# Mixture-of-experts decoder step: shift rows added by VectorE, and the last expert's rows picked on TensorE while the other experts' rows are gathered

## The reference

```python
    x = x + g1 * mixed
    h2 = (rms_norm(x, p['norm2_w']) * (1 + sc2) + sh2).reshape(bt * s, D_MODEL)
    comb = route(h2, w_router, router_bias)
    y_moe = moe_ffn(h2, comb, p['w_exp_gate'], p['w_exp_up'], p['w_exp_down']).reshape(bt, s, D_MODEL)
    x = x + g2 * y_moe
...
    y_prompt = rms_norm(xp, final_norm_w)
    y_sample = rms_norm(xs, final_norm_w)
```

## Time and profile before

| | us |
|---|---|
| median of 3 runs | 1065.74 (1063.61 to 1066.46) |
| the profiled execution | 1060.38 |
| its span from first to last instruction | 1058.6 |
| TensorE busy in that span | 987.4 (93%) |
| VectorE, ScalarE, GpSimd busy | 378.1, 234.0, 145.5 |
| last matmul of the last expert begins | about 1024.1 |

### The profile page before, as it was taken

How to read it: one execution, slowest core, us unless ns; L and a number is a source line. 1 busy time by engine, 2 the same in 40 slices (tenths; PEclk the granted TensorE clock), 3 DMA queues, 4 the chain that set the end, 5 groups by cost and what they waited for, 6 DMA issues and landing times.

```text
span 1058.6 us, 20482 instructions
## 1 busy us (share of the span) xinstructions
PE 987.4 (93%) x8640; PEld 751.7 (71%) x8640; DVE 378.1 (36%) x831; ACT 234.0 (22%) x465; POOL 145.5 (14%) x230
## 2 busy tenths in 40 slices
PE   4999999999989899999999999999799999999960
PEld 2667676676756566666666677666699999999960
DVE  3121235666436985666441610223011010010106
ACT  2130222332352322322241100014111011110003
POOL 0000233342000542243200000002000000000004
PEclk8999999999999999999999999998899999999995
DMA  9853346457354565656534533432749999999944
GB/s 381 306 197 119 122 157 226 142 199 244 126 185 160 184 223 200 199 183 213 180 126 146 202 122 123 153 119 93 266 173 402 396 411 397 395 414 399 403 167 141
DMA packets 47444, 238.03 MB, mean 225 GB/s; under 512 B 6832, under 2 KB 11472, under 8 KB 24080
## 3 DMA queue, kind: packets, MB, share of 16 engines
q1 hardware_dynamic: 45568, 231.63, 58.8%
q0 software_dynamic: 1472, 5.24, 1.5%
q10 hardware_dynamic: 336, 0.20, 0.1%
HBM read 212.31 MB, written 24.75 MB: 224 GB/s over the span
## 4 chain that ended last, share of the span: by engine, by line
PE 87%; DVE 3%; ACT 3%; issue 3%; DMA 2%; POOL 1%; SPq 0%; ACTq 0%; POOLq 0%; DVEq 0%
PE pjB L811 14%; PE pjA L811 14%; PE states L1364 11%; PE pjA L1202 7%; PE pjB L1202 7%; PE states L1367 5%; PE pjA L1364 3%; PE pjB L1364 3%; PE pjB L1367 2%; PE pjA L1367 1%; PE states L820 1%; PE bank L1166 1%; PE bank L935 1%; PE states L1181 1%; PE states L935 1%
## 5 line engine op out<-in xcount | busy, mean ns | idle before, releaser
L811 PE MATMUL pjB<-hF,ring 128*128 128x320 f32 x608 | 173.4, 439 | 0.0
L811 PE MATMUL pjA<-hF,ring 128*128 128x320 f32 x608 | 171.9, 436 | 0.5 <-ACT regA L1553 0.5
L1367 PE MATMUL states<-ring,oF 128*32 128x384 f32 x1392 | 154.8, 491 | 0.0
L1364 PE MATMUL states<-ring,oF 128*32 128x128 f32 x1392 | 154.8, 273 | 0.0
L1364 PEld LDWEIGHTS states<-ring,oF 128*32 128x32 f32 x1392 | 150.7, 110 | 2.6 <-issue 2.6
L811 PEld LDWEIGHTS pjB<-hF,ring 128*128 128x128 f32 x608 | 114.3, 192 | 49.2 <-issue 5.7
L811 PEld LDWEIGHTS pjA<-hF,ring 128*128 128x128 f32 x608 | 113.2, 190 | 50.7 <-issue 7.0
L2486 DVE TENSOR_TENSOR oF<-oF,states 128x384 f32<-128x384 f32 x16 | 8.9, 555 | 168.6 <-PE states L1367 168.6
L2243 DVE TENSOR_TENSOR G<-G 128x320 f32<-128x320 f32 x32 | 46.6, 1495 | 0.0
L1863 POOL TENSOR_TENSOR G<-regA,G 128x128 f32<-128x128 f32 (+1 forms) x32 | 19.0, 595 | 196.4 <-ACT G L1609 196.4
L1367 PE MATMUL pjB<-ring,hF 128*32 128x384 f32 x384 | 44.7, 491 | 0.0
(11 more groups left out here) (476 smaller groups left out, 1444.1 us busy)
## 6 DMA issues: line engine op xcount, KB each, us to landing
ring<-in_w SPq DMA_DIRECT2D x171, 1024.0 KB, 6.9
G<-in_ss SPq DMA_DIRECT2D x16, 512.0 KB, 4.0
out_ss_new<-G SPq DMA_DIRECT2D x16, 512.0 KB, 2.8
G<-csd SPq DMA_DIRECT2D x16, 320.0 KB, 3.5
yd<-hF SPq DMA_DIRECT2D x16, 288.0 KB, 6.0
G<-in_sg SPq DMA_DIRECT2D x4, 1024.0 KB, 6.4
out_sg_new<-G SPq DMA_DIRECT2D x16, 256.0 KB, 2.9
rF<-in_w SPq DMA_DIRECT2D x2, 1024.0 KB, 9.3
```

What stands on the lines that cost most here:

```text
L811: mm = pe.matmul(pj[g % 2][:, 0:T], w[:, k, half * P:half * P + P], hF[:, k, :], start=(k == 0), stop=(k == KT - 1))
L1364: pe.matmul(bank[CAP:P, c * P:(c + 1) * P], rows(c, True), w[:, WIDE:512], start=first and c == 0, stop=last, tile_position=(0, CAP), skip ...
L1367: mm = pe.matmul(bank[QUAD * c:QUAD * c + QUAD, 0:WIDE], rows(c, False), w[:, 0:WIDE], start=first, stop=last, tile_position=(0, QUAD * c) ...
```

## The change

It has three parts.

1. **Router and token rows.** `turn_u` now uses transposes; `turn_shift` is gone. Sixteen matmuls make the shift rows in two groups, those of the samples in `pjA` and `pjB` and those of the prompt in two other banks (ScalarE spreads the sample vectors to `shX` some 120 us earlier). ScalarE copies the shift rows straight into `hT`, and VectorE multiplies each turned bank by the norm's factor and adds it to `hT`, in six instructions that stand behind `idx` in its order. The pieces now come two halves of a tile after another, and POOL's three waits fit that. `ranks` on PE comes after the six turns as before.
2. **Loop.** `turn_act(e)` stands between the two halves of `down(e - 1)`, with two buffers for the turned activations. For the last expert the order is `down(14)`, `gate_up(15)`, `turn_act(15)`, `down(15)`; the order of the weights follows.
3. **End.** Expert 14's rows are stored from ScalarE's queue, and POOL gathers as soon as they have landed; expert 15 has no rows in `yd`, and its place in the two gathered sums counts with weight 0. A matrix with each token's weight for expert 15 at its row's place (`selT`, 96 x 320) is made ahead on VectorE and PE, and after `last_down()`, which now gives 96 plain rows of 512, PE multiplies by it (`picked`) so that expert 15's rows come out in token order. `plus` adds `hT` by the identity in the same bank. The residual is added by VectorE, not POOL; the tiles end in the order 0, 2, 1. The `conv_new` store moves from the end to just before the row loads.

```diff
-        if e:
+        if e and e < E - 1:
             out += [("down", e - 1, 0), ("down", e - 1, 1)]
+        if e == E - 2:
+            out += [("down", e, 0), ("down", e, 1)]
...
-TURNS = [(0, 0), (1, 0), (2, 0), (0, 1), (1, 1), (2, 1)]
+FINAL = [0, 2, 1]
+TURNS = [(0, 0), (0, 1), (1, 0), (1, 1), (2, 0), (2, 1)]
...
+            sp.dma_start(d["conv_new"], ncv[:, :, :]).then_inc(s_out, 16)
...
-                y_out(E - 1, 0, (E - 1) % 2)
...
-                    pe.matmul(turn_bank[n][0:rows, k * P:k * P + P], hF[:, 4 * half + k, c0:c1], ident,
-                              start=(k == 0), stop=False, skip_group_check=True)
+                    mm = pe.transpose(turn_bank[n][0:rows, k * P:k * P + P], hF[:, 4 * half + k, c0:c1], ident)
+                mm.then_inc(s_ht, 1)
...
-                flat_mod = mod[:, :, :].rearrange("p a q -> p (a q)")
                 for k in range(KT):
-                    at = (24 + k) * NSEQ
-                    for q in range(4):
-                        mm = pe.matmul(b[4 + k // 4][QUAD * q:QUAD * q + QUAD, k % 4 * P:k % 4 * P + P],
-                                       flat_mod[:, at:at + QUAD], ident, start=True, stop=True, tile_position=(0, QUAD * q))
+                    mm = pe.matmul(pj[k // 4][0:NSAMP, k % 4 * P:k % 4 * P + P], shX[:, k, :], ident, start=True, stop=True)
                 mm.then_inc(s_ht, 1)
-
-            def turn_shift(n):
-
-                t, half = TURNS[n]
-                c0, c1, rows = TT[t]
-                q = SHIFT_QUAD[n] * QUAD
-                left = s9[q:q + NSEQ, :] if t == 2 else rst[q:q + 1, c0:c1]
-                pe.matmul(turn_bank[n][0:rows, :], left, shR[q:q + left.shape[0], 512 * half:512 * half + 512],
-                          start=False, stop=True, tile_position=(q, 0), skip_group_check=True).then_inc(s_ht, 1)
+                for k in range(KT):
+                    mm = pe.matmul(b[4 + k // 4][:, k % 4 * P:k % 4 * P + P], mod[:, 24 + k, 0:1].to_broadcast([P, P]), ident,
+                                   start=True, stop=True)
+                mm.then_inc(s_ht, 1)
...
-            turn_u(2)
-            pe.wait_ge(s_rta, 3)
-            turn_u(3)
-            turn_u(4)
-            pe.wait_ge(s_rst, 3)
-            for n in range(4):
-                turn_shift(n)
-            pe.wait_ge(s_rst, 5)
-            turn_u(5)
-            turn_shift(4)
-            turn_shift(5)
+            for n, copied in ((2, 2), (3, 3), (4, 5), (5, 7)):
+                pe.wait_ge(s_rta, copied)
+                turn_u(n)
...
+            pe.wait_ge(s_dsp, DISPATCH_SEL - 1)
+            for t, (c0, c1, rows) in enumerate(TT):
+                mm = pe.transpose(b[2][0:CAP, c0:c1], selS[0:rows, t, :], ident[0:rows, 0:rows])
+            mm.then_inc(s_rank, 1)
+            pe.wait_ge(s_dsp, DISPATCH_SEL)
...
+                    if turn and h == 0:
+                        turn_act(turn[0])
...
+            def last_down():
+
+                pe.wait_ge(s_hev, XROWS // P + E)
+                act_ = actT[:, (E - 1) % 2]
+                for h in range(2):
+                    w = moe_chunk(pe, E - 1, 4 + h)
+                    pe.wait_ge(s_eyv if h else s_eya, E - 1)
+                    for k in range(BLOCKS):
+                        pe.matmul(pj[h][0:CAP, :], act_[:, k, 0:CAP], w[:, k, :], start=(k == 0), stop=False,
+                                  skip_group_check=True)
+                    for c in range(BLOCKS):
+                        mm = pe.matmul(pj[h][QUAD * c:QUAD * c + QUAD, :], act_[:, c, CAP:P], w[:, 3, :], start=False,
+                                       stop=True, tile_position=(0, QUAD * c), skip_group_check=True)
+                    mm.then_inc(s_used, 1)
+
+            def picked(t, h, last):
+
+                c0, c1, rows = TT[t]
+                out = (states[:, h], b[4 * h], states[:, 2 + h])[FINAL.index(t)]
+                pe.wait_ge(s_eya if t == 2 else s_eyv, E + h)
+                return pe.matmul(out[0:rows, :], selT[:, c0:c1], (yL if t == 2 else yLg)[:, h * 512:h * 512 + 512],
+                                 start=True, stop=last, skip_group_check=True)
+
+            def plus(t, h):
+
+                c0, c1, rows = TT[t]
+                out = (states[:, h], b[4 * h], states[:, 2 + h])[FINAL.index(t)]
+                return pe.matmul(out[0:rows, :], ident[0:rows, 0:rows], split(hT[0:rows, t, :])[:, h],
+                                 start=False, stop=True, skip_group_check=True)
...
+                def last(e, v):
+                    down(e, 1)
+                    pe.wait_ge(s_hea, e)
+                    gate_up(e, v)
                     turn_act(e)
 
-                experts(pe, one)
-                down(E - 1, 0)
+                experts(pe, one, last)
+                last_down()
+                picked(0, 0, True)
+                picked(2, 0, False)
+                picked(1, 0, False)
+                picked(0, 1, True).then_inc(s_yt, 1)
+                picked(2, 1, False)
+                pe.wait_ge(s_gm, 1)
+                for h in range(2):
+                    mm = plus(2, h)
+                mm.then_inc(s_yt, 1)
...
-            act.wait_ge(s_rst, 5)
-            for n, (t, half) in enumerate(TURNS):
+            for t, half in ((2, 0), (2, 1), (0, 0), (1, 0), (0, 1), (1, 1)):
                 rows = TT[t][2]
-                act.wait_ge(s_ht, n + 2)
-                act.activation(hT[0:rows, t, half * 512:half * 512 + 512], (b[3], pj[0], pj[1], b[4], b[5], b[0])[n][0:rows, :],
-                               ACT.Copy, scale=r3[0:rows, t:t + 1]).then_inc(s_htc, 1)
+                act.wait_ge(s_ht, 3 if t < 2 else 2)
+                act.activation(hT[0:rows, t, half * 512:half * 512 + 512], (pj if t == 2 else b[4:6])[half][0:rows, :],
+                               ACT.Copy).then_inc(s_rta, 1)
...
+                    act.dma_start(d["yd"][e - 1][:, 0:2 * WIDE], yE[0:CAP, 1 - v]).then_inc(s_yd[1 - v], 16)
+                    act.dma_start(d["yd"][e - 1][:, 2 * WIDE:D].rearrange("(b i) c -> i b c", b=BLOCKS),
+                                  yE[CAP:P, 1 - v].rearrange("p (b c) -> p b c", b=BLOCKS)).then_inc(s_yd[1 - v], 16)
...
+                experts(act, one, last)
+                act.activation(spare, eps, ACT.Sqrt)
+                weighted(0)
+                last_half(0)
+                weighted(1)
+                last_half(1)
+                weighted(2)
...
-                pool.wait_ge(s_htc, 4 + t)
+                pool.wait_ge(s_htc, 2 * t + 2)
...
-                    pool.wait_ge(s_yd[v], 32 * (E // 2))
+                    pool.wait_ge(s_yd[v], 32 * (E // 2 - v))
...
+            dve.wait_ge(s_rta, 7)
+            for n, (t, half) in enumerate(TURNS):
+                rows = TT[t][2]
+                dve.wait_ge(s_ht, 3 + n if n else 1)
+                y_ = hT[0:rows, t, half * 512:half * 512 + 512]
+                dve.scalar_tensor_tensor(y_, (b[3], b[0], pj[0], pj[1], b[4], b[5])[n][0:rows, :], r3[0:rows, t:t + 1], y_,
+                                         ALU.mult, ALU.add).then_inc(s_htc, 1)
...
+            dve.tensor_tensor_scan(iota, ones[:, 0:CAP], ones[:, 0:CAP], 0.0, ALU.mult, ALU.add).then_inc(s_cmb, 1)
+            dve.wait_ge(s_cmb, 1)
+            for t in range(3):
+                ds_(dve.tensor_scalar(selS[:, t, :], iota, rL[:, t:t + 1], comb[:, t * E + E - 1:t * E + E],
+                                      ALU.is_equal, ALU.mult))
+            dve.wait_ge(s_rank, 2)
+            dstep(dve.tensor_copy(selT, b[2][0:CAP, 0:T]))
...
+                rows = summed(0)
+                cm(gated(0, rows))
+                cm.wait()
+                cm(residual_rows(0, rows))
+                gated_half(0)
+                rows = summed(1)
+                gated_half(1)
+                cm(gated(1, rows))
+                dve.wait_ge(s_w1, 3)
+                dve.scalar_tensor_tensor(hT[0:NSAMP, 2, :], y2[0:NSAMP, 2, :], sel[0:NSAMP, 1, 8:9],
+                                         hT[0:NSAMP, 2, :], ALU.mult, ALU.add).then_inc(s_gm, 1)
+                cm.wait()
+                residual_rows(1, rows).then_inc(s_gm, 1)
+                dve.wait_ge(s_yt, 1)
+                dve.tensor_tensor(split(hT[:, 0, :]), states[:, 0:2, :].rearrange("p h (j i) -> p h j i", i=P),
+                                  split(hT[:, 0, :]), ALU.add).then_inc(s_x3, 1)
+                dve.wait_ge(s_yt, 2)
+                for h in range(2):
+                    cm(dve.tensor_tensor(split(hT[0:NSAMP, 2, :])[:, h], b[4 * h][0:NSAMP, :].rearrange("p (j i) -> p j i", i=P),
+                                         split(gT[0:NSAMP, 1, :])[:, h], ALU.mult))
+                cm.wait()
+                residual_rows(2, NSAMP).then_inc(s_x3, 1)
+                for n, t in enumerate(FINAL):
+                    final(n, t, True)
```

(7 more changed lines are left out.)

204 lines of the change are left out of this document (133 added, 71 removed).

## The result

| | before | after |
|---|---|---|
| median of 10 runs each, us | 1065.65 (1060.34 to 1066.85) | 1056.01 (1049.97 to 1058.80) |
| ratio, with its 95% interval | | 0.9912 (0.9895 to 0.9929) |
| the profiled execution; its span, us | 1060.38; 1058.6 | 1058.15; 1055.8 |
| the layer itself, up to the router's last square sum but one | 708.2 | 713.5 |
| from there to the first row turn | 37.8 | 31.0 |

The forecast was 1042.8 us; the measured time lies 6 us above the upper end of its range (1037 to 1050). The gain is 9.6 us where 22.9 were worked out. The two profiled executions differ by 5.25 us before the change's first instruction: the code there is the same, but TensorE's clock fell in the layer at different places (PEclk over 350 to 400 us was 1.00 before and 0.93 after). So stages are compared here, not absolute times.

A forecast was written before the change was run, and what follows sets the result against it. The prediction took TensorE itself to bound the experts, so gains had to come before or after them: 10.5 us at the start plus 12.4 at the end, 22.9 off the 1065.7 median, giving 1042.8 us, range 1037 to 1050.

The forecast's parts named there:

- Part 1, up to the first turn: Router and token rows: the first row turn comes at 739.3 instead of 745.96, a gain of 6.7 us.
- Part 1, the clock: First turn and expert 0: TensorE's clock stays full instead of half, 3.8 us more (bounds 0 and 3.8).
- Rival (a): Start: the clock stays low into expert 0, 3.8 us less gain, 1046.6 us; chance 0.18.
- Part 2, the loop: Expert loop: same instructions and same number of changes of form, the turn's new place hidden, so no gain or loss.
- The 0.7 for the exposed product and turn of expert 15: Last expert: VectorE's product and the turn are no longer covered before down(15), costing 0.7 us.
- Part 3, the store: End: expert 14's store takes 5 us beside the last two weight loads; the first gather pair lands 6.65 later, at 1020.2.
- rival (b): End: expert 14's store lands after 7.8 us and shifts the whole end, 2.8 us less gain, 1045.6 us; chance 0.15.
- Part 3, the chain to the end: From the first gather landing: VectorE and ScalarE in turn take 22.6 us, then 3.4 for the last store.
- the products on TensorE at half clock: End: sign that would refute the prediction if it held the end; at half clock the products would be 2 us late.
- the three changes of form: Last expert: down(15) pays three more changes between narrow and whole form at 0.45 us each, done at about 1028.5.

The follow-up runs named there:

- start_warm: The changed kernel with unused matmuls added in TensorE's idle times around the first row turn; 1050.8 us, ratio 0.9864.
- all_three: The changed kernel with the edits of both, start_warm's added matmuls and two more in the idle time left at the start; 1045.3 us, ratio 0.9806.
- halves_first: The changed kernel with expert 15's two halves ahead of the gathered rows in VectorE's and ScalarE's order; 1049.4 us, ratio 0.9862.
- store_sp: The changed kernel with expert 14's rows stored from SP's queue behind the last loads, not from ScalarE's; 1057.5 us, ratio 0.9921.
- tail_warm: The changed kernel, order kept, with five unused matmuls in TensorE's 4.8 idle us after last_down; 1051.2 us, ratio 0.9869.
- chunk_held: The changed kernel with the last 1 MB weight load held until expert 14's rows have landed; 1049.8 us, ratio 0.9859.
- both_warm: The changed kernel with the edits of both, start_warm's added matmuls and three more before the first plus; 1045.1 us, ratio 0.9828.
- both: The changed kernel with the last load held and expert 15's halves earlier: first before the first gathered sum, second behind tile 0's gate; 1048.5 us, ratio 0.9857.

## Why the prediction was wrong

**Part 1, up to the first turn: right.** 6.8 us against 6.7, by two small errors that cancel: the first scatter was 0.8 later than forecast (725.2 for 724.4, less the 5.25), which put the load 0.7 later; and TensorE, which I had as the last to be ready, was there before it.

**Part 1, the clock: wrong, 4.3 us.** "If TensorE goes from the banks to the turn with 2 us of thin work, the clock should stay up" failed. TensorE had no thin work there but 2.9 us of nothing, and later 0.9 us waits between the turns. The clock came back early for the turn and fell behind it, twice. start_warm and all_three show that the clock's fall goes with the idle times: filled, the same stretch takes 4.2 us less. Rival (a), low clock into expert 0, was priced at 3.8, but the first fall cost only 1.6 (halves_first, which has no second one, takes 32.6 us where the filled kernels take 31.0). The second fall, in the row turns between experts 0 and 1, cost 2.6, and neither the forecast nor a rival had it. It doesn't come in every execution, and what decides that is open.

**Part 2, the loop: right.** 215.5 us both times. The 0.7 for the exposed product and turn of expert 15 was right as well (0.73).

**Part 3, the store: wrong, 6.1 us.** "The last two weight loads go out at the same time as this store, so I take 5" failed: the second part took 9.8, beyond my bound of 7.8 from the earlier trace rows, and the first gather pair 7.4 instead of 6.65. The loads beside it set this: with one of them held the store took 6.9. From SP's queue it took 10.4 (store_sp). By the rule of the Trainium skill named in rival (b) (DMA: Bandwidth & Descriptors, "Issuing engines are not separate DMA queues") a store from ScalarE's queue runs on the same 16 DMA engines as the loads and interleaves with them. The traces agree that the queue doesn't matter much: 9.8 us from one, 10.4 from the other. I gave rival (b) a chance of 0.15, and the price I put on it (2.8) was that of the traffic before, where the store did not meet two loads.

**Part 3, the chain to the end: wrong, 4.8 us.** The 22.6 us of VectorE and ScalarE became 27.4. "The ten matmuls of 512 columns (0.9 each) fit" is the step: the sum listed "half of expert 15 0.7" behind four passes of VectorE and ScalarE and never asked what TensorE did meanwhile. I had named the sign ("the products on TensorE at half clock") and its price as 2 us. halves_first, tail_warm and chunk_held remove this loss in three ways. A smaller term was too large without harm: `down(15)` took 7.5 us, not 9.0, so the three changes of form that I had added to it (1.35) weren't there.

6.1 and 4.8, less 0.3 for a shorter last store, and 4.3 make 14.9; 22.9 - 14.9 = 8.0 us, which is what the stages show. The remaining 1.6 to the 9.6 of the medians is not explained; the runs spread more than that with the layer's clock. Rival (b) came true and rival (a) in part; together they would have given 1049.4 us. What the range lacked was the loss at the end, a larger price for the store, and the second fall of the clock in place of most of the first.

## What to carry to other kernels

When work moves off TensorE's path, write down TensorE's own row of idle times after the change, and price everything behind each of them at both clocks; a chain on VectorE that releases TensorE late costs little as a wait here (21.6 us from the landing in tail_warm, which keeps the order, and 20.3 in halves_first, which changes it) but 5.8 us as half clock behind it. An instruction that releases TensorE goes first in its engine's order, ahead of longer work for the same end. A transfer that is moved forward meets other traffic than where it was: price it by the traffic at its new place, and if it gates the end, hold back a load that has time.

## What was not expected of the hardware

VectorE's product of expert 15, a multiplication that reads one operand from SBUF and one from PSUM, started 1.1 to 3.5 us after its last input when POOL was issuing indirect gathers, and 0.1 us after it when they were made to wait. By what path they meet is open. Late loading of instructions is a rival that no run tests. An instruction transfer (queue q14) ran at 1015.8 us in all_three and at 1015.1 in both_warm, 0.4 and 1.1 us before the late product. But in chunk_held and both, where the product was 1.1 us late, none ran in the 5 us before it. It isn't VectorE's work beside POOL's as such: in halves_first `gated_half(0)` started on time (1014.34, TensorE's last matmul at 1014.28) while POOL issued one of these transfers (1013.73 to 1014.67). The Trainium skill (SBUF — State Buffer, "SBUF: two separate sides") names one point where the two engines block each other, a shared port pair that VectorE needs for its two-port modes or, against GpSimd work that reads SBUF, for two operands from SBUF. This product has only one, so the page gives no reason for the delay that these runs show.

TensorE's clock in the layer took two courses with the same code: the router's last square sum but one was at 708.2 us in the profile of before and at 713.5 in that of the changed kernel. The executions of the changed kernel with more of the full clock are the shorter ones (mean clock 0.979 at 1050.0 us, 0.971 at 1058.8); in other kernels it goes mostly so (not in all_three: 0.981 at 1045.6 us, 0.985 at 1047.8). So one profile can be 5 us off its median before the changed code is reached.
